# Routing one chunk of tokens at a time, with all places ahead of the shared expert's second weights on TensorE

## What is computed

```python
scores = sigmoid(h @ router_w)                      # (T, 64)
_, idx = top_k(scores + router_bias, 8)
gate = take_along_axis(scores, idx); gate = gate / gate.sum(-1) * 2.5
# every (token, expert) pair gets a place in its expert's list
out[slot] = (silu(x[slot] @ w_gate[e]) * (x[slot] @ w_up[e])) @ w_down[e]
routed = sum over a token's 8 experts of gate * out
shared = (silu(h @ sh_gate) * (h @ sh_up)) @ sh_down
h += g_f * (routed + shared)
```

## Time and profile before

| | |
|---|---|
| three runs | 2950.36, 2959.13, 2961.50 us |
| the profiled execution | 2956.34 us, of which the span is 2954.6 us |
| PE busy | 85% of the span |
| DVE, ACT, POOL busy | 41%, 21%, 23% |
| mean granted clock of PE | 0.917 |
| routing of layer 0, `lg_exp` to the first gather | 838.95 to 922.45 us |
| routing of layer 1 | 2262.40 to 2310.19 us |

### The profile page before, as it was taken

How to read it: one execution, slowest core, us unless ns; L and a number is a source line. 1 busy time by engine, 2 the same in 40 slices (tenths; PEclk the granted TensorE clock), 3 DMA queues, 4 the chain that set the end, 5 groups by cost and what they waited for, 6 DMA issues and landing times.

```text
span 2954.6 us, 43826 instructions
## 1 busy us (share of the span) xinstructions
PE 2497.5 (85%) x14732; PEld 1683.9 (57%) x14733; DVE 1199.4 (41%) x2349; ACT 631.6 (21%) x1140; POOL 667.9 (23%) x686
## 2 busy tenths in 40 slices
PE   5999788886866989999997598898867798999995
PEld 2348677776733555555554245787766455555552
DVE  4532576766261222222221543477664222222223
ACT  1125332322010111111111114523230111111111
POOL 0000253532013222222221000235321222222221
PEclk8999788988878999999999799999788899999998
DMA  6634000001152999999996352200016499999994
GB/s 257 256 132 90 1 1 1 1 1 34 46 222 96 367 353 358 348 336 333 365 349 217 131 199 71 47 1 1 1 34 246 167 367 362 367 365 358 381 351 148
DMA packets 188878, 573.16 MB, mean 194 GB/s; under 512 B 56543, under 2 KB 99879, under 8 KB 149831
## 3 DMA queue, kind: packets, MB, share of 16 engines
q1 hardware_dynamic: 162150, 520.29, 47.2%
q0 software_dynamic: 26592, 51.11, 7.1%
HBM read 552.37 MB, written 53.53 MB: 205 GB/s over the span
## 4 chain that ended last, share of the span: by engine, by line
PE 61%; DVE 13%; DMA 13%; issue 6%; ACT 2%; DVEq 2%; POOLq 1%; another core or an unknown queue 1%; ACTq 1%; SPq 1%; POOL 0%
PE ps L1659 56%; DMA featT<-ffn_rows,idx_in 7%; PE ps L1663 5%; DVE R L1064 4%; DMA R<-in_exp_down 4%; DVE featT L1064 1%; ACT R L807 1%; DVE R L1337 1%; DVE ring L1064 1%; POOLq L723 1%; DMA R<-in_w_mod 1%; ACT L807 1%; DMA R<-ffn_sum_even 1%; DVEq L1061 1%
## 5 line engine op out<-in xcount | busy, mean ns | idle before, releaser
L1659 PE MATMUL ps<-R 128*64 128x256 f32 (+5 forms) x9040 | 1427.7, 385 | 112.1 <-issue 49.4
L1659 PEld LDWEIGHTS ps<-R 128*64 128x64 f32 (+2 forms) x9040 | 884.7, 168 | 521.9 <-issue 284.7
L807 ACT ACTIVATE R<-ps 128x256 f32<-128x256 f32 (+3 forms) x395 | 175.4, 444 | 1197.9 <-PE ps L1659 1052.5
L1064 DVE TENSOR_TENSOR R<-R,ps 128x256 f32<-128x256 f32 (+2 forms) x250 | 137.3, 549 | 564.1 <-ACT R L807 500.4
L1659 PE MATMUL ps<-featT,ring 128*128 128x512 f32 (+1 forms) x768 | 312.4, 564 | 1.1 <-ACT R L807 0.8
L1659 PE MATMUL ps<-ring,R 128*128 128x128 f32 (+2 forms) x1200 | 262.4, 355 | 35.9 <-DMA ring<-in_sh_down 20.1
L1659 PEld LDWEIGHTS ps<-ring,R 128*128 128x128 f32 x1200 | 209.3, 215 | 70.4 <-issue 47.0
L1663 PE MATMUL ps<-ident,featT 128*128 128x128 f32 x1120 | 163.3, 292 | 98.3 <-DMA featT<-ffn_rows,idx_in 59.6
L1659 PEld LDWEIGHTS ps<-featT,ring 128*128 128x128 f32 x768 | 147.9, 196 | 162.8 <-issue 156.1
L643 POOL TENSOR_TENSOR R<-ring,lev 128x512 f32<-128x512 f32 x56 | 73.9, 1319 | 680.6 <-DVEq L1299 292.9
L1067 DVE TENSOR_SCALAR R<-ps,idx_out 128x512 f32<-128x512 f32 x128 | 96.1, 751 | 300.4 <-PE ps L1659 300.4
(11 more groups left out here) (197 smaller groups left out, 1837.6 us busy)
## 6 DMA issues: line engine op xcount, KB each, us to landing
R<-in_exp_gate SPq DMA_DIRECT2D x128, 1024.0 KB
R<-in_exp_up SPq DMA_DIRECT2D x128, 1024.0 KB
R<-in_exp_down SPq DMA_DIRECT2D x128, 1024.0 KB
R<-in_w_mod SPq DMA_DIRECT2D x48, 1024.0 KB, 7.4
ring<-in_w_in SPq DMA_DIRECT2D x30, 1024.0 KB, 5.4
ring<-in_w_out SPq DMA_DIRECT2D x8, 1024.0 KB, 7.5
ffn_sum_odd<-zero SPq DMA_DIRECT2D x6, 512.0 KB, 8.4
ffn_rows<-X SPq DMA_DIRECT2D x6, 512.0 KB
```

The source lines that it names most:

```text
L807: do(C.activation(out_, in_, func, **kw), name)
L1064: do(V.tensor_tensor(out_, a, b, op), name)
L1659: return MM(out_, lhsT, rhs, start=start, stop=stop)
```

## The change

On DVE the routing runs chunk by chunk: each chunk goes from its top 8 to its addresses before the next begins, and signals `mask_ready` and `pay_ready` on its own. The places are read from PSUM directly (a bank per chunk, 4 + c), the copy `pos` is gone, and so are the memsets (now POOL's, after `y_ready`) and the copy of `tokid` (also POOL's). The copies of the transposed tokens go from DVE to ACT, and PE's transposes go from behind `flag_ready` to right behind the logits. There are four buffers for them, `frow`, in place of the two of `X`. On PE the order is: transposes, first half of `sh_gate`, places of the first chunk, second half of `sh_gate`, places of all other chunks, `sh_up`, down products. POOL scatters a chunk as soon as that chunk's `pay_ready` comes, and loads the table without waiting for the down products (`tabA` has moved to where nothing is read); the wait for all stores stands behind the first three gathers.

```diff
@@ GpSimd @@
-                wait("blank_ready", 1, l)
+                nl = len(LIVE[l])
+                wait("y_ready", nl, l)
+                do(G.memset(blank[:, :, 1:2], 0.0))
+                do(G.memset(blank[:, :, 0:1].bitcast(I32), SKIP))
...
+                do(G.tensor_copy(pay[:, LIVE[l][0] * TOPK:, 0].bitcast(I32).rearrange("p (c k) -> p c k", c=nl),
+                                 tokid[:, LIVE[l][0]:].unsqueeze(2).to_broadcast([P, nl, TOPK])))
                 wait("blank_dram", 16, l)
-                wait("pay_ready", 1, l)
...
+                for n, c in enumerate(LIVE[l]):
+                    wait("pay_ready", n + 1, l)
+                    for k in range(c * TOPK, (c + 1) * TOPK):
+                        pool.indirect_dma_start(rows, ...)
                 wait("tab_dram", 16 * nl * TOPK, l)
-                wait("shd_ps", nl, l)
-                wait("shd_sb", nl, l)
                 pool.dma_start(tabA[:, :, :], tab_dram[0:P, :, :]).then_inc(S["tab_loaded"], 16)
-                wait("tab_loaded", 16, l)
-                wait("acc_zeroed", 16 * nl, l)
+                wait("flag_ready", 1, l)
                 for b in range(2):
-                    wait(f"x_stored{b}", 16 * nl, l)
+                    wait(f"x_stored{b}", 16 * (nl // 2), l)
...
                 for s in range(3):
                     gather(s, s)
+                wait("acc_zeroed", 16 * nl, l)
+                for b in range(2):
+                    wait(f"x_stored{b}", 16 * nl, l)
@@ ScalarE, between the logits' exp and sh_silu @@
+                for n, c in enumerate(LIVE[l]):
+                    wait("ftok_ps", n + 1, l)
+                    f(frow[n].rearrange("p (k j) -> p j k", k=KT), bank(4 + 2 * (c % 2), 2)..., ACT.Identity, "ftok_sb")
@@ VectorE @@
-                do(V.memset(blank[:, :, 1:2], 0.0))
-                do(V.memset(blank[:, :, 0:1].bitcast(I32), SKIP), "blank_ready")
...
+                for n, c in enumerate(live):
+                    (max, max_index, if8, hots)
+                    do(V.tensor_reduce(mask[:, c, :], ...), "mask_ready")
+                    (s8, gsum, reciprocal, gates)
+                    wait("pos_ps", n + 1, l)
+                    tt(hot2[:, :, :], hv, eight(ps[:, 4 + c, 0:NE]), ALU.mult)
                     do(V.tensor_reduce(p8[:, c, :], hot2[:, :, :], AX.X, ALU.add))
+                    stt(dst8[:, c, :], p8[:, c, :], float(NE), if8[:, c, :], ALU.mult, ALU.add)
+                    cp(dsti[:, ks, 0], dst8[:, c, :], "pay_ready")
...
                 for n, c in enumerate(live):
                     wait("shd_ps", n + 1, l)
-                    wait(f"x_stored{c % 2}", 16 * (nl // 2 + n // 2), l)
-                    cp(X[:, c % 2, :], bank(4 + 2 * (c % 2), 2), "shd_sb")
+                    if n == 0:
+                        for b in range(2):
+                            wait(f"x_stored{b}", 16 * (nl // 2), l)
+                    cp(frow[n], bank(4 + 2 * (c % 2), 2), "shd_sb")
@@ TensorE @@
+                for n, c in enumerate(live):      # the transposes, from behind flag_ready
...
+                def places(x):
+                    c = live[x]
+                    wait("ftok_sb", nl, l)
+                    wait("mask_ready", x + 1, l)
+                    (masks times triS or ones into bank 4 + c; with the last chunk the counts into bank 7)
+                    ins.then_inc(S["pos_ps"], 1)
+
+                sh_half(0, 0)
+                places(0)
+                sh_half(0, 1)
+                for x in range(1, nl):
+                    places(x)
+                sh_half(1, 0)
+                sh_half(1, 1)
+
+                wait("flag_ready", 1, l)
```

More of the change, by code:

```diff
@@ L995, in _ @@
                 f(scor[:, cs, :], ps[:, 0, 0:NT * NE].rearrange("p (c e) -> p c e", c=NT)[:, cs], ACT.Exp, "lg_exp", scale=-1.0)
+                for n, c in enumerate(LIVE[l]):
+                    wait("ftok_ps", n + 1, l)
+                    f(frow[n].rearrange("p (k j) -> p j k", k=KT), bank(4 + 2 * (c % 2), 2).rearrange("p (j k) -> p j k", k=KT), ACT.Identity, "ftok_sb")
                 wait("sh_ps", 1, l)
@@ L1511, in _ @@
-                eight = lambda ap: ap.unsqueeze(1).to_broadcast([P, TOPK, NE])
-                for c in live:
-                    hv = hots[:, c, :].rearrange("p (k e) -> p k e", k=TOPK)
+                    cp(if8[:, c, :], i8[:, c, :])
                     tt(hv, eight(iota_e[:, :]), if8[:, c, :].unsqueeze(2).to_broadcast([P, TOPK, NE]), ALU.is_equal)
-                    do(V.tensor_reduce(mask[:, c, :], hots[:, c, :].rearrange("p (k e) -> p e k", k=TOPK), AX.X, ALU.add))
-                dve.drain().then_inc(S["mask_ready"], 1)
@@ L1542, in _ @@
                 do(V.tensor_copy(flagi[:, :], flag[0:1, 1:3]), "flag_ready")
-                for n, c in enumerate(live):
-                    wait("ftok_ps", n + 1, l)
-                    if n >= 2:
-                        wait(f"x_stored{c % 2}", 16 * (n // 2), l)
-                    cp(X[:, c % 2, :].rearrange("p (k j) -> p j k", k=KT), bank(4 + 2 * (c % 2), 2).rearrange("p (j k) -> p j k", k=KT), "ftok_sb")
                 wait("sh_silu", 1, l)
@@ L2045, in _, with sh_half @@
                     ins.then_inc(S["ftok_ps"], 1)
+                wait("lg_exp", 2, l)
+                def sh_half(n, half):
+                    m = N_IN + N_OUT + n
+                    ring_wait(m, l)
+                    for k in range(KT):
+                        ins = mm(ps[:, 2 * n + half, P * live[0]:], ring[:, m % 2, k, tk(half)], featT[:, k, P * live[0]:], k == 0, k == KT - 1)
+                    if half:
+                        ins.then_inc(S["sh_ps"], 1)
+                        pe.drain().then_inc(S["ring_used"], 1)
+                def places(x):
+                    c = live[x]
+                    wait("ftok_sb", nl, l)
+                    wait("mask_ready", x + 1, l)
+                    for c2 in live[:x + 1]:
+                        ins = mm(ps[:, 4 + c, 0:NE], triS if c2 == c else ones[:, :], mask[:, c2, :], c2 == live[0], c2 == c)
+                    for c2 in live if c == NT - 1 else ():
+                        ins = mm(ps[:, 7, NE:2 * NE], ones[:, :], mask[:, c2, :], c2 == live[0], c2 == NT - 1)
+                    ins.then_inc(S["pos_ps"], 1)
[7 more added lines that the diff above has]
+                wait("flag_ready", 1, l)
                 m = N_IN + N_OUT + 2
-                wait("ftok_sb", nl, l)
                 wait("sh_mul", 1, l)
```

63 lines of the change are left out of this document (18 added, 45 removed).

## The result

The changed kernel takes 2944.62 us, median of 11 runs (2935.99 to 2950.75), against 2960.80 us for the kernel before, 11 runs (2950.36 to 2969.83). The ratio is 0.9944, 95% interval 0.9928 to 0.9960: 16.2 us or 0.56% faster. I had forecast 2934 us and 22.9 us of gain. The measured time lies 10.6 us above the forecast, inside its range. The faster side was the right one, though by little: 0.56% stands just outside the 0.5% that I took as the bound, and the interval reaches inside it. The band that I called the forecast itself, 2929 to 2941 us, was missed by 3.6 us.

A forecast was written before the change was run, and what follows sets the result against it. PE's order was taken to set the end of the stage from the logits' exp to the first gather. Gains of 13.0 and 9.9 us, 22.9 together, off the profiled 2956.34 gave 2933.4, called 2934 us; range 2922 to 2955.

The forecast's parts named there:

- The sum: Stage from the logits' exp to the first gather: 13.0 us gained in layer 0, 9.9 in layer 1, 22.9 together.
- The reason given for layer 0's gain: Between `sh_up` and down products: copies (7.7 us), transposes and the wait for `sh_down` no longer stand there; 13.0 us gained.
- late releases: DVE going on after PE had finished by the records: 5.2, 13.1 and 2.6 us in layer 0 before, none in layer 1.
- The earlier scatters are hidden, and PE's order alone sets the end.: End of layer 0's stage: the table lands at 899.7, 8 us early, behind it DVE's last copy ends at 907.6.
- Late releases come back in part: Rival, at `sh_ps` 2 and first down products: one or two of 5 to 13 us; 2941 to 2952; chance 0.17.
- They strike the places: Rival, layer 0: five PE completions in the scatter window come late, `pos_ps` 2 to 4 among them; 2965 and more; 0.06.
- each late by L costs L, since DVE, then PE, stand for it: Layer 0, five PE completions under the scatters: gain gone at L = 4.6 us, over 0.5% slower at 7.5.
- Nothing arrives at the end: Rival, expert loops: bound partly by weight loads, they end where they did; 2955 to 2963 us; chance 0.07.
- the signs that I had named for being wrong: Down-product copies waiting for "remote", scatters beyond 1.5 us, or loop lengths differing by over 5 us.
- the short bound: ACT's strided copies of transposed tokens at 1.0 us each, giving 1.8 us back; short rival 2922 to 2928, chance 0.08.
- The clock of PE around the gap: Layer 0, PE idling about 12 us before the last places: clock falls to 0.50, `sh_up` takes 2.3 us more.
- The rule that speaks against it: Scatters beside DVE's routing might take 2.51 us each: gathers 4.3 and 3.0 us worse, 2941 us; chance 0.05.

The follow-up runs named there:

- few scatters: The changed kernel with one scatter per chunk instead of eight, leaving out seven of a token's eight experts; 2837.83 us, not comparable with full kernels.
- before_few_scatters: The kernel before with one scatter per chunk instead of eight, leaving out seven of a token's eight experts; 2847.22 us.
- early_transposes_alone: The kernel before with only early transposes, their copies on ACT and four buffers; routing and places stay one batch; 2944.27 us, ratio 0.9954.
- interleaved: The changed kernel with each half of `sh_up` put before one of the later places on PE; 2945.16 us, ratio 0.9950 to the kernel before.
- pause_each_chunk: The changed kernel with POOL waiting, before each chunk's eight scatters, until all earlier ones have landed; 2942.44 us, ratio 0.9942 to the kernel before.
- interleaved_pause: The changed kernel with `sh_up` halves before later places and POOL waiting for earlier scatters before each chunk's, both layers; 2939.11 us, ratio 0.9936 to before.
- held_scatters: The changed kernel with all scatters held back until `sh_up` is done, nothing left out; 2984.81 us in one execution.
- narrow_scatters: The changed kernel with all scatters kept, each writing 16 partitions instead of 128; 2853.27 us in one execution.

## Why the prediction was right, and where it was not

**The sum.** 70.55 and 37.9 us forecast, 70.8 and 38.1 with few scatters. With them 72.2 and 41.8. The missing 5.6 us (17.3 instead of 22.9) are 1.7 in layer 0 and 3.9 in layer 1. The median lies 10.6 us above the forecast; the rest is the scatter of single executions, from one of which (2956.34) the sum started. That layer 0's total came out within 1.7 us was in good part luck, as follows.

**The reason given for layer 0's gain was wrong.** The prediction said that the gain is that neither the copies, nor the transposes, nor the wait for `sh_down` stand between `sh_up` and the down products. They are gone, but in layer 0 what came instead is as long: PE's two gaps (4.91 and 5.84 us, 10.8 of the 12 forecast), places at the slow clock, and `sh_up` 1.8 us longer. `before_few_scatters` shows the balance: 0.5 us. The 13.0 of the sum were in truth two other things, each about half: the removal of the late releases, which I had written down as 5.2 and 13.1 us beside the sum and never as a term of it, and the earlier start of the scatters. The sum came out right because it went from the trace's own 922.45, in which both lay, to an end built up without them. That is the step that failed: a new end computed clean minus an old end that is not clean books the disturbance as gain of the edit. For layer 1, with no late release before, the reason stands: 9.3 us.

**"The earlier scatters are hidden, and PE's order alone sets the end."** Right for the new kernel by POOL's own times: the last scatter ends 60.7 us behind the exp (898.1, which is 2.31 us before the table load at 900.41), forecast 57.2, and the table waits, though 3.7 us and not 8. Wrong as a reason why their earlier start is worth nothing: the 7 us of slack in the kernel before were slack against copies that late releases had pushed back. Once PE's path is clean the scatters started at the old place end last, about 78 us behind the exp (`early_transposes_alone`), so their earlier start earned some 6 us. And wrong in effect, since they hold back what PE says to DVE.

**The rivals.** *Late releases come back in part* is what happened. I gave it 0.17, with one or two of 5 to 13 us and 2945 us as the centre; there were two, of 11.6 and 7.4, and the median is 2944.6. But their cost was not their length: 1.4 and 3.7 us. And its "against: none in layer 1" was no argument: under the scatters of the kernel before only the transposes ended there, 3 and 5 us into the run, while `sh_up` ended before it and the first down products (2300.01) with it (2300.0), so little could come late; the change has put the end of `sh_up` under them. *They strike the places* named the right place too: it was `pos_ps` 4. The failing step there is the rule "each late by L costs L, since DVE, then PE, stand for it". PE stands for DVE only up to the last mask. Behind the last places it has `sh_up`, 15.82 us, and DVE's delay of 11.6 ran under it; what showed was `sh_mul` 1.1 us late, because the counts and flags stood in front of it. `interleaved` is that rival in full: with the last places behind `sh_up` and its drain there is no such cover, and the stage is 7.4 us longer. *Nothing arrives at the end* is refuted by the loops, which kept their length within 0.9 us. Of the signs that I had named for being wrong, the loops did not show and DVE's copies of the down products did not wait for "remote"; its pick of the last places did instead, and one step of the scatters beside the routing of layer 0 stretched to 1.61 us, start to start.

**Terms.** ACT's strided copy: 1.97 us (3.94 for two), taken as 1.9; it was never near the 1.0 of the short bound. The clock of PE around the gap, by stretches of time of the changed kernel (columns: stretch, its length, busy time and instructions of PE, PE's loads, DVE, ACT and POOL, granted clock, DMA share, GB/s):

```profile
863.00:870.00 7.00, 1.32 (x6) 1.13 (x6) 5.95 (x16) 0.00 (x0) 5.25 (x6) 0.50 0.02 1
873.00:877.00 4.00, 4.00 (x8) 2.06 (x8) 0.00 (x0) 0.00 (x0) 3.08 (x4) 0.50 0.02 1
877.00:881.00 4.00, 4.00 (x10) 1.83 (x9) 0.00 (x0) 0.00 (x0) 3.09 (x4) 0.95 0.02 1
```

1.2 GHz in the gap and in the first 3.8 us of `sh_up` (0.95 over 877 to 881 is 0.50 until about 877.4), then 2.4 GHz: `sh_up` took 15.82 us for 14.0, 1.8 more, where I had 2.3. The last places took 3.65 us instead of 1.9 for the same reason, and that I had not counted. In compensation the down products took 13.97 us and not 14.4. `sh_down` in layer 1 was there 26.04 us behind the exp (PE's release with few scatters), forecast 25.0.

**The rule that speaks against it** did not bite: beside DVE's routing the scatters kept 1.28 us start to start, for instance 859.53, 860.81 and 862.08, all but the first step (1.39) and the scatter at 868.47, which took 1.31 us instead of 0.97 while DVE had just begun a comparison over all experts (868.24). The Trainium skill, SBUF — State Buffer, section "Who interferes with whom", by its exclusive port between GpSimd and DVE's 2-port instructions, left room for small casts only, and the trace agrees as far as it goes: the longest cast of the routing took 0.23 us, the others 0.17. The late releases fall while DVE stands idle.

## What to carry to other kernels

When the old end holds a wait that the trace can't resolve, build the old stage up clean as well, and compare clean with clean; the difference between the clean sum and the trace is a term of its own, and the edit earns it only if it moves the work out of its reach. A delayed signal costs what is left of it when its reader's own readers have run out of queued work, so count the cover behind each waiting instruction before multiplying. And a queue that is "hidden" by its own times can still be felt: try the kernel with an eighth of it before believing that it is off the path.

## What was new about the hardware

A run of indirect DMAs on POOL, 1.28 us apart, is accompanied by late signals of PE: raised 1.8 to 14.5 us after its matmuls had ended. Where a `drain` stands behind the signal, PE's next matmul is late with it (`interleaved`, 11.0 us). What the runs bound:

- With only one scatter in eight, none was late (three kernels). With a run cut every eight scatters by a wait for their landing, none was late in layer 0 (three kernels) nor in layer 1 of `pause_each_chunk`; in layer 1 of `interleaved_pause` `sh_ps` was raised 1.8 us late, and nothing waited for it. They stay when each scatter writes an eighth (10.6 and 11.0 us late).
- Age alone doesn't bound them. Under `held_scatters` everything in the first 14 us of a run was on time, and in the changed kernel `pos_ps` 3 was, 11 us into the run, while `pos_ps` 4, 21 us into it, was not. But `ftok_ps` 4 of the kernel before, 9 us into its run, came 2.6 us late, and `sh_ps` of layer 1 of `interleaved`, 7 us into its run, 3.8 us late.
- Nor does the end of a run release them. Some came just after it paused or ended (885.4 after 883.8 in the changed kernel), some several us later (914.1 after 909.5 in the kernel before, 889.9 after 884.1 in `narrow_scatters`), and some in its middle (880.2 and 902.8 in the kernel before, 892.3 in `early_transposes_alone`, 875.3 in `interleaved`, 2279.5 in the changed kernel).
- `narrow_scatters` shows DVE's own instructions held to one in 1.40 us for 11 us, so whatever is disturbed isn't PE's alone.

Whether it is the number of DMAs under way, their own completion signals, or POOL's work in issuing them is left open; no run here varied one of these without the others. And one plain price: ScalarE's copy from PSUM with a strided output took 1.97 us for 128x1024 float32, DVE's 1.95.
